# Sample attention: products of different sequences take turns on the column groups of the array, logits two sequences at a time

## The reference, cut to what matters

```python
# per sequence b: q (4 tokens, 8 heads, 64), keys and values: 256 of the cache and 4 new
idx    = _indexer_topk(q_i, w_i, k_i_all, t_pos, topk)          # which keys count
logits = jnp.einsum('bqhd,bqkhd->bqhk', q, k_sel) * 64 ** -0.5 + bias
p      = jax.nn.softmax(logits, axis=-1)
out    = jnp.einsum('bqhk,bqkhd->bqhd', p, v_sel)
```

## Time and profile before

| | before |
|---|---|
| median of 3 runs | 2203.22 us |
| the profiled execution, its own time | 2211.91 us |
| its span from first to last instruction | 2210.2 us |
| PE busy | 2096.9 us (95% of the span) |
| DVE, ACT, POOL busy | 1072.6, 627.2, 334.7 us |
| mean granted clock of PE | 0.963 |
| sample attention, first key transpose to first transpose of the GLA | 764.0 to 880.4 us |

### The profile page before, as it was taken

The page is one execution under the profiler, slowest core; times in us unless marked ns, Lnnn a source line. Parts: engine busy times, 40 slices in busy tenths (PEclk is TensorE's granted clock), DMA queues, the critical chain, the costliest instruction groups (busy, mean ns, idle before and its releaser), DMA issues. The chain is left out here.

```text
span 2210.2 us, 31133 instructions
## 1 busy us (share of the span) xinstructions
PE 2096.9 (95%) x12125; PEld 1873.6 (85%) x12125; DVE 1072.6 (49%) x2226; ACT 627.2 (28%) x1108; POOL 334.7 (15%) x294
## 2 busy tenths in 40 slices
PE   5999996999999999988889999999999999999997
PEld 4789996999999786777759987888998899889995
DVE  5489997345454330545554424444334432443245
ACT  4323221223333361444344313311212111111112
POOL 6512222333223121001013310000000000000000
PEclk7999998999999899998979999999999999999999
DMA  4202331222212242343344340211011110111002
GB/s 139 85 20 77 118 107 59 87 78 80 67 58 83 64 134 88 131 140 144 124 159 151 117 144 1 77 58 39 29 48 58 39 52 26 58 58 39 20 1 89
DMA packets 144139, 173.82 MB, mean 79 GB/s; under 512 B 9688, under 2 KB 120830, under 8 KB 143486
## 3 DMA queue, kind: packets, MB, share of 16 engines
q1 hardware_dynamic: 136158, 148.14, 20.6%
q0 software_dynamic: 7840, 23.67, 3.1%
HBM read 127.38 MB, written 44.40 MB: 78 GB/s over the span
## 5 line engine op out<-in xcount | busy, mean ns | idle before, releaser
L855 PE MATMUL ring<-n_hi,piece_hi 128*128 128x352 f32 (+1 forms) x1320 | 441.4, 334 | 1.1 <-DVE n_whole L1664 1.0
L857 PE MATMUL ring<-n_hi,piece_lo 128*128 128x352 f32 (+1 forms) x1320 | 429.5, 325 | 0.0
L856 PE MATMUL ring<-n_lo,piece_hi 128*128 128x352 f32 (+1 forms) x1320 | 429.1, 325 | 0.0
L1241 ACT ACTIVATE arena<-ring 128x352 f32<-128x352 f32 (+7 forms) x368 | 153.3, 438 | 483.6 <-PE ring L857 345.3
L2198 POOL TENSOR_TENSOR piece_lo<-piece_whole,piece_hi 128x1024 fp32r<-128x1024 f32 (+2 forms) x71 | 165.5, 2331 | 714.1 <-ACT piece_hi L1254 714.0
L855 PEld LDWEIGHTS ring<-n_hi,piece_hi 128*128 128x128 f32 (+1 forms) x1320 | 251.8, 191 | 9.0 <-issue 6.7
L856 PEld LDWEIGHTS ring<-n_lo,piece_hi 128*128 128x128 f32 (+1 forms) x1320 | 252.3, 191 | 0.6
L857 PEld LDWEIGHTS ring<-n_hi,piece_lo 128*128 128x128 f32 (+1 forms) x1320 | 251.2, 190 | 0.5
L1752 DVE TENSOR_SCALAR_CACHE_REDUCE arena<-arena 128x384 uint8<-128x384 f32 (+6 forms) x224 | 190.7, 875 | 1.4 <-DVE arena L1752 0.2
L856 PE MATMUL ring<-h_lo,gate_hi 128*128 128x352 f32 x528 | 170.7, 323 | 6.2 <-issue 6.2
L855 PE MATMUL ring<-h_hi,gate_hi 128*128 128x352 f32 x528 | 172.0, 326 | 0.0
(11 more groups left out here) (278 smaller groups left out, 3679.0 us busy)
## 6 DMA issues: line engine op xcount, KB each, us to landing
piece_whole<-w_in SPq DMA_DIRECT2D x54, 512.0 KB, 3.6
projected_rows<-arena SPq DMA_DIRECT2D x44, 528.0 KB, 2.7
arena<-projected_rows SPq DMA_DIRECT2D x12, 1056.0 KB, 5.0
gate_whole<-w_ffn_gate SPq DMA_DIRECT2D x11, 1024.0 KB, 5.2
up_whole<-w_ffn_up SPq DMA_DIRECT2D x11, 1024.0 KB, 5.3
down_whole<-w_ffn_down SPq DMA_DIRECT2D x11, 1024.0 KB, 4.7
arena<-projected_rows SPq DMA_DIRECT2D x16, 528.0 KB, 3.6
arena<-x_prompt SPq DMA_DIRECT2D x16, 512.0 KB, 5.2
```

The costliest lines, as they stand in the source:

```text
L855: pe.matmul(out, lhi, rhi, start=first, stop=False)
L856: pe.matmul(out, lhi, rlo, start=False, stop=False)
L857: return pe.matmul(out, llo, rhi, start=False, stop=last)
L1241: evacuates(act.activation(dst, src, ACT.Copy, scale=scale), *key)
```

## The change

On PE the sequences of a group are taken in two pairs. The keys of both sequences of a pair are turned (16 transposes, four chunks, all four banks of the ring), then both fillers run, then the logits of both: within each slice f the two sequences take turns, so that neighbouring matmuls lie on different column groups. `so_used` goes up by two behind the last of them. In "so" the page p is now the outer loop and the sequence j the inner one, and the four matmuls of the new tokens stand together at the end. No matmul is added or removed. On ACT the four key copies of a pair stand together, then follow the filler and the softplus of each, and the wait for `so_used` names the pair. `plan` follows PE.

```diff
@@ plan
-            for j in range(4):
-                for p in range(NPG):
-                    plan("kp", g, j, p)
-                plan_d(*sample_group(4 * g + j))
+            for j0 in (0, 2):
+                for j in (j0, j0 + 1):
+                    for p in range(NPG):
+                        plan("kp", g, j, p)
+                for j in (j0, j0 + 1):
+                    plan_d(*sample_group(4 * g + j))
@@ PE, logits
-                for j in range(4):
-                    b = 4 * g + j
-                    pe.wait_ge(ks_landed[b % 2], 32 * (b // 2 + 1))
...
-                    dense(*sample_group(4 * g + j))
-                    for p in range(NPG):
-                        wait_evac(pe, "kp", g, j, p)
-                    if j == 0:
+                for j0 in (0, 2):
+                    two = (j0, j0 + 1)
+                    for j in two:
+                        b = 4 * g + j
+                        pe.wait_ge(ks_landed[b % 2], 32 * (b // 2 + 1))
+                        for p in range(NPG):
+                            ps = begin("kp", g, j, p)
+                            for f in range(4):
+                                ins = pe.transpose(ps[:, f * P:(f + 1) * P], kpS[b % 2][:, p, f * P:(f + 1) * P], ident)
+                            done(ins, "kp", g, j, p)
+                    for j in two:
+                        dense(*sample_group(4 * g + j))
+                    for j in two:
+                        for p in range(NPG):
+                            wait_evac(pe, "kp", g, j, p)
+                    if j0 == 0:
                         pe.wait_ge(lg_used, len(UN))
                     for c0, cn in ((0, PAST), (PAST, DT)):
                         for f in range(4):
-                            rhs = kTs[b % 2][:, f, :] if cn == PAST else kdS[:, f, b * DT:(b + 1) * DT]
-                            ins = pe.matmul(lgt[g][32 * j:32 * j + 32, c0:c0 + cn], qbS[:, 4 * b + f, :], rhs,
-                                            start=f == 0, stop=f == 3)
-                    ins.then_inc(so_used, 1)
+                            for j in two:
+                                b = 4 * g + j
+                                rhs = kTs[b % 2][:, f, :] if cn == PAST else kdS[:, f, b * DT:(b + 1) * DT]
+                                ins = pe.matmul(lgt[g][32 * j:32 * j + 32, c0:c0 + cn], qbS[:, 4 * b + f, :], rhs,
+                                                start=f == 0, stop=f == 3)
+                    ins.then_inc(so_used, 2)
@@ PE, outputs
                 ps = begin("so", g)
-                for j in range(4):
-                    for p in range(NPG):
+                for p in range(NPG):
+                    for j in range(4):
                         pe.matmul(ps[32 * j:32 * j + 32, :], ptS[:, p, 32 * j:32 * j + 32], vpS[4 * g + j][:, p, :],
                                   start=p == 0, stop=False)
+                for j in range(4):
                     ins = pe.matmul(ps[32 * j:32 * j + 32, :], ptS[0:NS, 2, 32 * j:32 * j + 32], vd[0:NS, token_rows(NTP), :],
                                     start=False, stop=True)
@@ ACT
-                for j in range(4):
-                    b = 4 * g + j
-                    if b >= 2:
-                        act.wait_ge(so_used, b - 1)
-                    for p in range(NPG):
-                        copy_out(kTs[b % 2][:, :, p * P:(p + 1) * P],
-                                 bank("kp", g, j, p).rearrange("p (a b) -> p a b", a=4), "kp", g, j, p)
-                    staged(*sample_group(b))
-                    if b == 4:
-                        sample_exp(0)
-                    if b < GH:
-                        softplus(b)
+                for j0 in (0, 2):
+                    for b in (4 * g + j0, 4 * g + j0 + 1):
+                        if b >= 2:
+                            act.wait_ge(so_used, b - b % 2)
+                        for p in range(NPG):
+                            copy_out(kTs[b % 2][:, :, p * P:(p + 1) * P],
+                                     bank("kp", g, b % 4, p).rearrange("p (a b) -> p a b", a=4), "kp", g, b % 4, p)
+                    for b in (4 * g + j0, 4 * g + j0 + 1):
+                        staged(*sample_group(b))
+                        if b == 4:
+                            sample_exp(0)
+                        if b < GH:
+                            softplus(b)
```

## The result

The changed kernel takes 2184.16 us, the median of 4 runs (2182.88 to 2187.63), beside 2203.78 us for the kernel before in 4 runs on the same chip (2202.76 to 2206.76). The ratio is 0.9912, with an interval of 0.99 to 0.9925: faster by 19.6 us. The forecast was 2191.5 us, 11.7 us faster, in a range from 2186.

A forecast was written before the change was run, and what follows sets the result against it. PE, busy for 95% of the span, was taken to bound the kernel. "so" at -16.8 and the logits at +5.1 gave -11.7 us, from 2203.2 to 2191.5 us, in a range from 2186 to 2205.

The forecast's parts named there:

- The column groups run side by side: PE matmuls of the sample attention: instructions on different column groups overlap, and all gain hangs on this.
- Rival (1): Matmuls start in program order: "so" takes 6.2 us a chunk, gains 10.0 us for two; total 2198.3 us; chance 0.18.
- rival (2): Column groups take turns without overlap and the ring decides: 7.8 us slower, 2211.0 us; "so" 10.5 us; chance 0.12.
- "so", -16.8 us: Output chunks on PE: four column groups at a time take 2.81 us a chunk, not 11.22; two chunks gain 16.8 us.
- two changes, 0.23 us: In one sequence of "so", 0.23 us are lost at the two changes between 128-row and 32-row matmuls.
- The logits, +5.1 us: Sample logits in pairs: 8.3 us less streaming, 1.7 of old stalls, against about 10.8 of new stalls and 4.4 of clock.
- Edits at nothing: Key pages and the GLA's first rows still land in time, the softplus is used later: no cost.
- Rival (3): The gain of "so" is given back by a later load or ACT in the GLA, up to all: about 2203; chance 0.13.
- the sum without clock loss: Low end of the range: -16.8 us for "so" and +0.7 for the logits, a bit beyond: 2186 us.

The follow-up runs named there:

- Kernel 6: The changed kernel, but within a pair the logits of one sequence are all multiplied before the other's; 2192.39 us, ratio 0.9954.
- kernel 8: The kernel before with only the narrow 32-row matmuls of "so" moved into a loop of their own, wide ones still sequence by sequence; 2184.36 us, ratio 0.9917.
- kernel 3: The changed kernel with ACT's order alone changed: the next pair's key copies go ahead of a softplus that would hold the ring; 2177.53 us, ratio 0.9885.
- kernel 4: kernel 3 with POOL's low half of a weight piece moved behind the key pages of sequence 5; 2177.32 us, ratio 0.9874.
- kernel 7: The changed kernel with the wide matmuls of "so" taking turns over only two column groups at a time; 2184.05 us, ratio 0.9906.
- kernel 1: The kernel before with only the new loops of "so", logits as before; 2186.73 us, ratio 0.9914.
- Kernel 10: kernel 4 with 8 more transposes hidden ahead of a filler in the GLA, their result overwritten; 2172.12 us, ratio 0.9855.

## Why the prediction was right or wrong

**The column groups run side by side: right.** This was the point on which all gain hung, and it was read from two nearly equal rows. Rival (1), program order and 6.2 us a chunk, and rival (2), no overlap and 10.5, are both out at 2.85. The Trainium skill, TensorE: Matmul & The Clock Gate, section Part 3: Packing small matmuls, has matmuls start and end strictly in program order; kernels 6 and 8 show matmuls on a free column group starting ahead of earlier ones on a busy one, so here the measurement decides. The same section's 2.38 times for three column tiles is not contradicted but goes further here: four give 11.22 / 2.85 = 3.9 times, a part of it because two changes of row size stand in the chunk instead of eight.

**"so", -16.8 us: right in size.** 2.85 us for a forecast of 2.81. C, which holds both chunks, is 16.7 us shorter. The reason given, turns taken among groups, was wrong in one part: turns are not needed. It is enough that no 32-row matmul stands between the wide ones (kernel 8). The forecast read "two changes, 0.23 us" as a small cost of its own; that the same change kept the next column group from starting was in the earlier trace rows all along, as four equal stretches that never overlapped while the four groups were free.

**The logits, +5.1 us: right in mechanism, 1.1 us too much.** The pair's logits took 2.07 us for 2.1. The stalls were 5.28 and 4.19 us for 5.3 and 5.5, at the places named, behind softplus(1) and softplus(3), and kernel 3 shows that ACT's order makes them: with that alone changed, both are gone and B is 10.2 us shorter. The second was shorter than forecast, and its clock dearer: the half clock covered 4.13 and 6.11 us of PE's work, half of which is lost, 5.1 us where 4.4 were taken. One part of this hadn't been thought of: the second half clock starts at 794.60, with PE at work, 2.5 us ahead of the stall, so part of the work ahead of a stall was slowed as well. Filler 8 starts 68.4 us behind the first key transpose, for a forecast of 69.6; before it was 64.4.

**Edits at nothing: the key pages and the GLA's first rows, right.** No wait for either in the changed kernel. Kernels 3 and 4 show the cover that was named: without the stall, the pages of 5 are late by 2.73 us, and the low half on POOL is why.

**The failed step: all behind "so" was taken as unchanged.** The prediction closes its edits at nothing with the GLA's first rows and "The softplus of ACT and DVE is used after that", and its sum ends where the GLA begins: it has no term for the GLA. The GLA came out 7.0 us shorter (266.1 to 259.1). That is 7.0 of the 7.9 us that the sum missed; most of the rest is the 1.0 us too much in the logits. No instruction there was removed or moved; what differs is 16.2 us less of half clock (59.9 to 43.7). Half of that, 8.1 us, is an estimate of what it can cost, and PE was busy for 7.2 us less. Over 18 profiled executions of 14 programs the length goes with where the clock falls at the GLA's first wait:

- falls 0.46 us or more ahead of the matmul that ends the wait: D is 258.4 to 262.1 us, 7 executions
- falls later than that, 0.26 us ahead up to 0.62 behind: 265.7 to 269.2, 10 executions
- one at 1.16 us behind: 264.1

In all 10 executions of the second kind, and in the last one, the clock falls again 34 us behind the first fall; in the 7 short ones it doesn't, and the next fall comes 65 us behind the first. The second fall by itself is about half of the 7 us: of the 16.2 us of half clock it holds 6.8, and the rest comes from one more fall and a longer one late in the GLA. The first profile of the pairs alone lacks the second fall but has the late ones, 53.3 us of half clock in all, and its D is 262.05. So it is shown that the 7 us are time at half clock. What puts the first fall on one side or the other is not. It isn't the change as such, since the pairs alone show either, "so" alone has runs that spread over 9.4 us, and kernels 3 and 8 over 9 as well; the changed kernel in its two profiles and "so" in twos in its one fell on the short side, and by their times their other runs did too. An attempt to set it by the amount of work ahead hit in two profiles and missed in one. In the changed kernel the short GLA repeats, but as no run shows why, its 7.0 of the 19.6 us are luck and not something that the edit was made for.

Rival (3) looked at this place but only in one direction: it had the GLA give a gain back. The range's low end, "the sum without clock loss", counted the clock in the stage that was changed and in no other. The profile before has 64.9 us of half clock in the GLA alone, so a gain or a loss of some us there was a term to be bound from both sides.

## What to carry to other kernels

Small matmuls that fill only some columns of the array run side by side on their column groups if nothing of another row size stands between them and no group gets more than four instructions in a row (an f32 matmul is two); moving one such matmul out of the loop can be worth more than any interleaving. When PE bounds a kernel, an edit that shifts its start by a few us can also shift where the clock falls in later stages, so give stages behind the edit a term of their own, of both signs, from the time at half clock they hold. And before pairing work on PE, see whose program feeds it: here the pairing cost 4 us of its stage until ACT's copies went ahead of its long work, and the change would have been better without it.

## What the runs showed of the hardware that was not expected

**Room for four.** As these runs look, a column group takes four instructions, one that runs and three that wait, before it blocks what follows. Kernel 6 suggests it by the start of the second sequence at the fifth instruction of the first (0.89 us), and the earlier trace rows agrees, where the next sequence starts with the fifth of the one before. Kernels 7 and 8 show that four have room; how the limit moves with other shapes wasn't tried.

**A second fall of the clock out of full work.** 34.1 us behind the first one in the GLA, after 27.22 us of work in 27.30 us (rows of the kernel before, second profile, and of kernel 1). In 7 of 18 executions it is missing.

**Three pauses in the FFN that vanish.** In the kernel before, PE waits three times for nothing that the view of waits names, some 144 us apart (1689.8, 1834.2 and 1978.4 us). That view (time in all, times, longest) from 1400 to 2150 us, and the row after the first of them:

```profile
PE ring L856 <- issue: 6.2, 3, 2.1
```

```profile
1691.99 0.33 PE L856 MATMUL ring<-h_lo,gate_hi 128*128 128x352 f32 x1 [2.15 <-issue]
```

With 8, 14 or 24 more PE instructions ahead of them, in the sample keys or in the GLA, they are gone, in all five kernels that have the additions, and E is 6 to 8 us shorter than in the same kernel without. The one with 8 hidden transposes over the same part:

```profile
1143.62:2196.00 1052.38, 1030.48 (x5725) 0.99 0.18 58
```

2197.88 us is 6.5 us less than before for work that is thrown away. The traces tell what goes with the pauses. PE's FFN is a loop of four passes of 792 matmuls (`pe.Fori`), so its program jumps back three times, and each pause stands ahead of the fifth matmul after such a jump: the same three matmuls in all 13 executions that have pauses. The row of the DMA view for loads of program code (packets of 16 KB, MB, share of 16 engines), from 1400 to 2150 us, in the kernel before and then in the one with 8 hidden transposes:

```profile
q8 instruction: 41, 0.67, 0.4%
```

```profile
q8 instruction: 15, 0.25, 0.1%
```

Over the whole program these loads are 105 in each of the 13 executions with pauses and 78 in each of the 5 without; the 27 that are gone are nine for each of the three passes after the first. In the profile ahead one of them starts at 1689.25 us, 0.2 us after the second pass has begun, and the pause begins 0.6 us later. So the pauses go with the loop's program being loaded again for every pass. A mere shift in time is out: the second pass begins at 1685.38 us in the second profile of the kernel before, which has the pauses, and at 1685.21 with the 8 hidden transposes, which has none. Why a few instructions ahead of the loop decide whether it is loaded again isn't shown. Kernel 10, the fastest one here, has them gone too.
